# Stick-breaking attention on one NeuronCore: one activation table for Exp and Ln block by block, and the four heads as one run of 48 blocks

## What is computed

```python
def stick_breaking_attention(q, k, v):
    for blk in range(t_len // SB_BLOCK):          # SB_BLOCK = 128
        z = jnp.einsum('bhtd,bhsd->bhts', qb, kb).astype(jnp.float32) * scale
        causal = s_idx < t_idx
        log_beta = jax.nn.log_sigmoid(z)
        log_one_minus = jnp.where(causal, jax.nn.log_sigmoid(-z), 0.0)
        tail = lax.cumsum(log_one_minus, axis=3, reverse=True) - log_one_minus
        weights = masked_exp(causal, log_beta + tail)
        outs.append(jnp.einsum('bhts,bhsd->bhtd', weights, vb.astype(jnp.float32)))
```

## Time and profile before

| | before |
|---|---|
| median of three runs | 5353.64 us (5345.07 to 5355.42) |
| profiled execution, time | 5354.07 us |
| its span | 5351.9 us |
| TensorE busy (PE) | 4827.9 us, 90% of the span |
| VectorE busy (DVE) | 2726.8 us, 51% |
| ScalarE busy (ACT) | 1057.5 us, 20% |
| stick-breaking stage, first matmul to last `finish` | 2076.30 to 2495.19 us of the span |

### The profile page before, as it was taken

The page is one execution under the profiler, slowest core; times in us unless marked ns, Lnnn a source line. Parts: engine busy times, 40 slices in busy tenths (PEclk is TensorE's granted clock), DMA queues, the critical chain, the costliest instruction groups (busy, mean ns, idle before and its releaser), DMA issues. The chain is left out here.

```text
span 5351.9 us, 43527 instructions
## 1 busy us (share of the span) xinstructions
PE 4827.9 (90%) x16184; PEld 2473.9 (46%) x16184; DVE 2726.8 (51%) x3797; ACT 1057.5 (20%) x1562; POOL 379.3 (7%) x251
## 2 busy tenths in 40 slices
PE   8988788899999798888987989988999988999996
PEld 3434443344444344333653334436888843444442
DVE  6546554745555532223534564544344355666767
ACT  1003321200000001333322021232433421110101
POOL 0015311000000000001211000000000010000000
PEclk9999899999999899988998999997999989999998
DMA  2221202111111122111123022443112021111112
GB/s 100 81 94 44 83 32 110 63 47 39 48 46 64 68 79 79 40 41 68 55 95 112 32 106 87 158 159 93 43 36 51 18 110 64 40 47 40 44 43 79
DMA packets 191862, 366.20 MB, mean 68 GB/s; under 512 B 102975, under 2 KB 104527, under 8 KB 190888
## 3 DMA queue, kind: packets, MB, share of 16 engines
q1 hardware_dynamic: 175720, 319.92, 17.7%
q0 software_dynamic: 7872, 28.84, 1.5%
q10 hardware_dynamic: 8064, 14.68, 0.7%
HBM read 264.65 MB, written 98.73 MB: 68 GB/s over the span
## 5 line engine op out<-in xcount | busy, mean ns | idle before, releaser
L172 PE MATMUL mlp_bank<-mlp_u,mlp_s 128*128 128x512 f32 x864 | 381.9, 598 | 5.4 <-DVEq L256 5.4
L172 PE MATMUL p_bank<-p_t,p_s 128*128 128x512 f32 x720 | 319.3, 600 | 11.7 <-DVEq L885 11.7
L172 PE MATMUL mlp_bank<-mlp_x,mlp_s 128*128 128x512 f32 x608 | 273.3, 592 | 0.0
L172 PEld LDWEIGHTS mlp_bank<-mlp_u,mlp_s 128*128 128x128 f32 x864 | 166.1, 193 | 216.8 <-issue 213.3
L236 ACT ACTIVATE mlp_p<-mlp_bank 128x512 f32<-128x512 f32 x70 | 41.4, 591 | 953.9 <-PE mlp_bank L172 929.8
L172 PEld LDWEIGHTS p_bank<-p_t,p_s 128*128 128x128 f32 x720 | 138.0, 192 | 188.7 <-issue 187.1
L246 DVE TENSOR_TENSOR mlp_sum_u<-mlp_bank,mlp_p 128x512 f32<-128x512 f32 x70 | 48.4, 692 | 308.1 <-PE mlp_bank L172 306.9
L172 PEld LDWEIGHTS mlp_bank<-mlp_x,mlp_s 128*128 128x128 f32 x608 | 115.5, 190 | 145.4 <-issue 140.4
L172 PE MATMUL mlp_bank<-tail_z,mlp_s 128*128 128x512 f32 x352 | 158.2, 592 | 0.0
L236 ACT ACTIVATE p_p<-p_bank 128x512 f32<-128x512 f32 x30 | 17.9, 597 | 677.8 <-PE p_bank L172 677.8
L628 ACT ACTIVATE mlp_cv<-mlp_raw,mlp_taps 128x1024 f32<-128x1024 f32 x44 | 54.6, 1240 | 455.4 <-DVEq L643 455.4
(11 more groups left out here) (742 smaller groups left out, 9339.0 us busy)
## 6 DMA issues: line engine op xcount, KB each, us to landing
mlp_w<-in_w_up SPq DMA_DIRECT2D x38, 512.0 KB
proj<-p_ev SPq DMA_DIRECT2D x38, 512.0 KB, 3.6
p_w<-in_w_in SPq DMA_DIRECT2D x28, 512.0 KB, 5.8
first_w<-in_w_in SPq DMA_DIRECT2D x24, 512.0 KB, 4.1
hgnx_merge_g<-proj SPq DMA_DIRECT2D x8, 1536.0 KB, 7.2
tail_mlp_w<-in_w_up SPq DMA_DIRECT2D x22, 512.0 KB
p_w<-in_w_out SPq DMA_DIRECT2D x16, 512.0 KB, 4.4
mid_mlp_w<-in_w_up SPq DMA_DIRECT2D x16, 512.0 KB
```

The source lines that it names most:

```text
L172: mm = nc.tensor.matmul(self.bank[product - 1][:, :], lhs[:, p, :], rhs(name, p), start=p == 0, stop=p == kp - 1)
```

## The change

Only `stick_breaking` is changed, in four ways.

1. ScalarE runs block by block: decay(n), weight(n-3), logarithm(n). The gate's Sigmoid of the next head moves to block 6 of the head before, and behind each Sigmoid a load of the table set `natural_log_exp_and_others` is written out, so Exp and Ln share a table.
2. The heads run as one sequence of 48 blocks on all three engines: TensorE's score(n+3) and values(n-3) cross from one head to the next, and `finish` of a head's second half comes at block 3 of the next.
3. V has a buffer for each head, so `keep` no longer waits for the heads before; the values of heads 2 and 3 are turned within head 1 (`turn` at blocks 4 and 7, `keep` at 7 and 10).
4. TensorE's wait for `padded` moves behind the first four quarters, and `take` moves behind `logw`.

The bodies of score, tail, decay, logarithm, weight, soft, sum_up, logw, finish and take are the same (they move out of a loop), and so is the number of quarters in each block step.

```diff
@@ -2009,7 +2009,7 @@
-        V = [r.sb(f"v{s}", [P, KD, HD]) for s in range(2)]
+        V = [r.sb(f"v{h}", [P, KD, HD]) for h in range(H)]
...
@@ -2087,7 +2087,6 @@
                 for sem in (tail_ready, pv_done):
                     pe.sem_inc(sem, 3)
-                pe.wait_ge(padded, 1)
                 def gate_quarter(m):
...
@@ -2114,71 +2113,78 @@
                 for m in range(STICK_AHEAD):
                     gate_quarter(m)
-                for i in range(H // 2):
...
-                    for s in range(2):
-                        h = i * 2 + s
-                        if s == 0:
-                            turn(i, 0)
-                        pe.wait_ge(loaded[s], (i + 1) * 48)
-                        pe.wait_ge(q_scaled, h + 1)
+                pe.wait_ge(padded, 1)
...
+                    nc.tensor.matmul(O[:, a:], V[h][:, b, :], weights(n)[:, a:], start=first(n), stop=b == 0)\
+                      .then_inc(pv_done, 1)
+
...
+                def begin(h):
+                    pe.wait_ge(loaded[h % 2], (h // 2 + 1) * 48)
+                    pe.wait_ge(q_scaled, h + 1)
+
+                turn(0, 0)
+                for at in range(H * NB + 3):
+                    if at == 0:
+                        begin(0)
                         for n in range(3):
-                            score(h, s, n)
-                        for n in range(NB + 3):
-                            if n + 3 < NB:
-                                score(h, s, n + 3)
-                            if n < NB:
-                                tail(h, n)
-                            if n == 1 and s == 0:
-                                turn(i, 1)
-                            m = STICK_AHEAD + 4 * STICK_SHARE * h + n
-                            if n < 4 * STICK_SHARE and m < 4 * STICK_TILES:
-                                gate_quarter(m)
-                            if n == 3:
-                                pe.wait_ge(v_ready, 2 * i + 2)
-                            if n >= 3:
-                                values(h, s, n - 3)
+                            score(0, 0, n)
+                    h, n = divmod(at + 3, NB)
+                    if h < H:
+                        if n == 0:
+                            begin(h)
+                        score(h, h % 2, n)
+                    h, n = divmod(at, NB)
+                    if h < H:
+                        tail(h, n)
+                    if at == 1:
+                        turn(0, 1)
+                    if h % 2 and n in (4, 7) and h + 1 < H:
+                        turn((h + 1) // 2, n // 7)
+                    if STICK_AHEAD + at < 4 * STICK_TILES:
+                        gate_quarter(STICK_AHEAD + at)
+                    h, n = divmod(at - 3, NB)
+                    if at >= 3:
+                        if h % 2 == 0 and n == 0:
+                            pe.wait_ge(v_ready, h + 2)
+                        values(h, h % 2, n)
...
                 def keep(i, half):
                     act.wait_ge(v_turned, 2 * i + half + 1)
-                    if half == 0:
-                        act.wait_ge(pv_done, done(2 * i, -1))
                     for s in range(2):
-                        ins = nc.scalar.activation(V[s][:, half * (KD // 2):(half + 1) * (KD // 2), :],
+                        ins = nc.scalar.activation(V[2 * i + s][:, half * (KD // 2):(half + 1) * (KD // 2), :],
                                                    TV[:, :, s * HD:(s + 1) * HD], ACT.Copy)
                     ins.then_inc(v_ready, 1)
...
-                    for s in range(2):
-                        h = i * 2 + s
-                        if s == 0:
-                            keep(i, 0)
-                        act.wait_ge(loaded[s], (i + 1) * 48)
-                        nc.scalar.activation(SG[s][:, :], G[s][:, :], ACT.Sigmoid).then_inc(sig_ready, 1)
-                        for g in range(0, NB + 3, 3):
-                            for n in range(g, min(g + 3, NB)):
-                                decay(h, n)
-                            for n in range(max(g - 3, 0), g):
-                                weight(h, n)
-                            for n in range(g, min(g + 3, NB)):
-                                logarithm(h, n)
-                            if g == 0 and s == 0:
-                                keep(i, 1)
...
+                def gate_sigmoid(h):
+                    act.wait_ge(loaded[h % 2], (h // 2 + 1) * 48)
+                    nc.scalar.activation(SG[h % 2][:, :], G[h % 2][:, :], ACT.Sigmoid).then_inc(sig_ready, 1)
+                    nc.scalar.preload_act_table_set("natural_log_exp_and_others")
+
+                gate_sigmoid(0)
+                keep(0, 0)
+                for at in range(H * NB + 3):
+                    if at < H * NB:
+                        decay(*divmod(at, NB))
+                    if at >= 3:
+                        weight(*divmod(at - 3, NB))
+                    if at < H * NB:
+                        logarithm(*divmod(at, NB))
+                    if at == 2:
+                        keep(0, 1)
+                    h, n = divmod(at, NB)
+                    if n == 6 and h + 1 < H:
+                        gate_sigmoid(h + 1)
+                    if h % 2 and n in (7, 10) and h + 1 < H:
+                        keep((h + 1) // 2, n // 10)
...
-                    if i == 0:
-                        for half in range(STICK_AHEAD // 2):
-                            take(half)
-                    for s in range(2):
-                        h = i * 2 + s
-                        for n in range(NB):
-                            soft(h, n)
-                            if n % 2 == 0 and 0 < n <= 4 * STICK_SHARE:
-                                take(STICK_AHEAD // 2 + 2 * STICK_SHARE * h + n // 2 - 1)
-                            sum_up(h, n)
-                            if n % 3:
-                                logw(h, n - 1)
-                            if n % 3 == 2:
-                                logw(h, n)
-                            if n == 7:
-                                finish(h, s, 0)
-                        if 4 * STICK_SHARE >= NB:
-                            take(STICK_AHEAD // 2 + 2 * STICK_SHARE * (h + 1) - 1)
-                        finish(h, s, 1)
...
+                for half in range(STICK_AHEAD // 2):
+                    take(half)
+                for at in range(H * NB):
+                    h, n = divmod(at, NB)
+                    soft(h, n)
+                    if h and n == 3:
+                        finish(h - 1, (h - 1) % 2, 1)
+                    sum_up(h, n)
+                    if at:
+                        logw(*divmod(at - 1, NB))
+                    if at and at % 2 == 0:
+                        take(STICK_AHEAD // 2 + at // 2 - 1)
+                    if n == 7:
+                        finish(h, h % 2, 0)
+                logw(H - 1, NB - 1)
+                finish(H - 1, (H - 1) % 2, 1)
```

More of the change, by code:

```diff
@@ new lines, in _, with score @@
+                pe.wait_ge(padded, 1)
+                def score(h, s, n):
+                    g, b = todo[n]
+                    z, q_ = Z[n % 3], Q[s][:, g * HT:(g + 1) * HT]
+                    keys = K_[s][:, b * P:(b + 1) * P]
+                    pe.wait_ge(lb_ready, done(h, n - 3))
+                    a = start(n)
+                    if diagonal(n):
+                        nc.tensor.matmul(z[:, a:a + P], keys, q_[:, a:a + P], start=True, stop=False)
+                        mm = nc.tensor.matmul(z[:, a:a + P], ident[:, :], before[:, :], start=False, stop=True)
+                        a += P
+                    if a < HT:
+                        mm = nc.tensor.matmul(z[:, a:], keys, q_[:, a:], start=True, stop=True)
+                    mm.then_inc(z_ready, 1)
@@ new lines, in tail @@
+                def tail(h, n):
+                    pe.wait_ge(sp_ready, done(h, n))
+                    pe.wait_ge(logw_ready, done(h, n - 2))
+                    a, t, s_ = start(n), TL[n % 2], soft_[n % 3]
+                    e = a + P if diagonal(n) else a
+                    if e > a:
+                        mm = nc.tensor.matmul(t[:, a:e], later[:, :], s_[:, a:e], start=True, stop=True)
+                    if e < HT:
+                        nc.tensor.matmul(t[:, e:], later[:, :], s_[:, e:], start=True, stop=False)
+                        pe.wait_ge(run_ready, done(h, n - 1))
+                        mm = nc.tensor.matmul(t[:, e:], ones[:, :], run[(n - 1) % 3][:, e:], start=False, stop=True)
+                    mm.then_inc(tail_ready, 1)
@@ new lines, in values @@
+                def values(h, s, n):
+                    g, b = todo[n]
+                    pe.wait_ge(w_ready, done(h, n))
+                    if first(n):
+                        pe.wait_ge(y_ready, y_done(h, g) - 1)
+                    a = 0 if first(n) else start(n)
+                    nc.tensor.matmul(O[:, a:], V[h][:, b, :], weights(n)[:, a:], start=first(n), stop=b == 0)\
```

(36 more changed lines are left out.)

114 lines of the change are left out of this document (22 added, 92 removed).

## The result

| | before | after |
|---|---|---|
| median (runs) | 5354.53 us (4: 5345.07 to 5356.88) | 5267.88 us (4: 5260.52 to 5277.89) |
| ratio, 95% interval | | 0.9843, 0.9822 to 0.9863 |
| profiled execution, time and span | 5354.07, 5351.9 us | 5266.99, 5264.7 us |
| first score to last `values` | 400.7 us | 316.7 us |
| waits of TensorE in it | 49.1 us, 16 | none |

The kernel is 86.7 us faster by the medians and 87.1 us by the profiled executions; the four runs after spread over 17 us. The busy time by stretch of TensorE, cut as the earlier trace rows are (length, busy time, granted clock), shows where from. The three stretches are: first quarter to first score, first score to last `values`, and all that comes after the stage.

What follows compares the result with a forecast made beforehand. TensorE, busy for 90% of the span, was taken as the bound, losing time to stalls and half clock. Profiled 5354.07 less 49.1 (stalls), 35.6 (half clock) and 1.4 (late wait) gave 5268 us, range 5258 to 5294.

Steps and rivals of the forecast that it cites:

- TensorE's own work: Stage from first score to last `values`: TensorE's work at 2.4 GHz, 82.5 us a head, 316 us for four heads.
- The check by one full block: TensorE's full block step, 7.40 us from `values` to `values`, set beside 82.5 / 12 = 6.9 us for the mean block.
- Stalls and half clock: TensorE in the stage: all 16 stalls, 49.1 us, and 35.6 us of half clock were to go.
- The late wait: Stage start: with the wait for `padded` moved, TensorE starts 1.1 to 1.7 us earlier, taken as 1.4 us.
- What hides the new work: ScalarE: two loads and a Sigmoid a head, 3.6 us, fit inside its 10 us to spare; the gate's fetch comes in time.
- small gaps: Rival: VectorE's order makes `soft` 1.0 us late after each of 24 `take`; 24 us come back, 5292 us; 9 in 100.
- shared-table failure: Rival: Exp and Ln still load a table each in every block on ScalarE; 5276 us; 4 in 100.
- exposed round trip: Rival: TensorE waits each step for Abs, Exp, `weight`, Ln and `soft`, 10.4 us a step; 5453 us; 3 in 100.
- The price of 8 us for unshared tables: With two loads a block, ScalarE's 5.0 us against 2.9 shows only in the last four blocks, 8 us.
- the head starts' stall: At each head's start, a stall of up to 5.3 us, counted in the 49.1 us, goes with one run of 48 blocks.
- the lead of "some 10 us": ScalarE's chain to `soft`: it ends some 10 us before TensorE asks for it, so all 16 stalls should go.
- VectorE standing at `take`: VectorE waits at `take` for quarter n-1; costs nothing, as `soft`(n+1) is needed only after a whole TensorE step.

## Why the prediction was right

The prediction was 5268 us, the measured median is 5267.9. That they agree to 0.1 us is luck, with runs that spread over 17 us. The sum holds in its terms, though, and not only in its total.

- **TensorE's own work.** 316 us from length times clock over the slow stretches; measured 316.69. The check by one full block held too.
- **Stalls and half clock.** 49.1 + 35.6 = 84.7 us were to go; 84.0 went. All 16 waits are gone and the clock is 1.00.
- **The late wait.** 1.4 us; measured 1.36, and the variant with the wait in front has 6.82 us again.
- **Not in the sum.** 1.9 us from the stages before, 0.55 us after the stage and 0.7 us given back at its start, in all 1.8 us of gain in code that was not changed. It is within the spread.
- **What hides the new work.** Two loads and a Sigmoid, 3.66 us, lie inside ScalarE's idle time. The fetch of a later head came in time: for head 2 the gate was issued at 2196.19, which with the 5.0 us of the earlier trace rows is some 2.5 us before its Sigmoid at 2203.68. ScalarE waited for a gate once, 3.1 us, for head 0 at the stage's start, where TensorE was at the early quarters and saw nothing of it (timeline of ScalarE).

```profile
2078.76 1.06 ACT L2225 ACTIVATE stick_sg<-stick_g 64x1024 f32<-64x1024 f32 x1 [3.05 <-DMA stick_g<-proj]
```

- **Rivals.** No small gaps, no shared-table failure, no exposed round trip. The price of 8 us for unshared tables was in the wrong place: the last four blocks hide them, the first block doesn't (1.6 us).

Two reasons in it were off, and neither could be seen from the total. First, I put the head starts' stall down to the merge of the heads and the rest to block by block with one table. The runs show that the order inside the head (with V for each head and the place of `keep`) does 69 of the 83 us in the stage alone, the shared table is needed for at most 16 of what is left, and the merge for nothing once the table is shared: without it the stage is 338.6 us. The change has two cures for the same last 10 to 16 us. Second, the lead of "some 10 us". I took it from ScalarE's chain; with one step of 5.4 to 7.4 us taken away TensorE stalls 31 times, so in the blocks behind a `take` or a `finish` the lead is under one step. I had named VectorE standing at `take` and called it harmless on the strength of one whole step. That was enough: a step less a stall of 0.4 to 2.2 us leaves, by an estimate from these runs, some 3 to 7 us there.

## What to carry to other kernels

Where an engine waits for a batch on another engine, look at how late the first item of the batch comes, not at what the batch saves: grouping three logarithms, with what went with it here, saved 64 table loads of 1.28 us on an engine that was idle for most of the stage, and cost 69 us on the one that was the bound. Price a stall on TensorE with the half clock behind it, and take the engine's own work as busy time times granted clock; here that gave the new time of the stage to 1 us. Once TensorE waits for nothing, look for matmuls to take off it: with the mask on VectorE the stage was another 15 us shorter, while 203 us more of work on ScalarE cost at most 8.

## What the runs showed of the hardware

Half clock behind stalls is dear and roughly in proportion to them: 34.3 us for 49.1 us of stalls, 16.3 for 28.2, 22.9 for 35.3 and 51.6 for 81.3, so 0.6 to 0.7 us for each. Each of these is one execution, and it isn't a rule for small sums: with 6.5 us of stalls in four pieces at the head starts it was 7.7. Single stalls don't follow it either. In the kernel before, the stall of 1.04 us in head 0 lies within a stretch at 1.00, and the one in head 1 is followed by a stretch at 0.76 (busy time by stretch; the clock stands behind the five engines):

```profile
2112.00:2146.00 34.00, 31.39 (x101) 15.20 (x100) 7.47 (x20) 14.70 (x27) 0.00 (x0) 1.00 0.09 32
...
2226.00:2233.00 7.00, 7.00 (x17) 3.17 (x15) 0.00 (x0) 2.30 (x3) 0.00 (x0) 0.76 0.00 0
```

And with the table shared, of two equal stalls of 2.02 us at the same place, one in head 0 and one in head 1, the first was followed by half pace and the second by full, as the lengths of the two pieces behind it show (timeline of TensorE):

```profile
2164.19 2.01 PE L2143 MATMUL stick_tl<-stick_sp,mid_later 128*128 128x512 f32 x2 [2.02 <-DVE stick_sp L2256]
...
2256.73 1.12 PE L2143 MATMUL stick_tl<-stick_sp,mid_later 128*128 128x512 f32 x2 [2.02 <-DVE stick_sp L2256]
```

What decides it was not tried and stays open. That stalls of 0.4 to 2.2 us, in 31 of 48 blocks, bring it on I had not expected.
